# Scaling half-finished softmax rows on GpSimd instead of VectorE in three attention stages of a four-layer backbone

## The reference, cut to what matters

```python
# layer 0: 16 query heads, 4 key/value heads; context queries see context keys only
s = einsum("bkgqd,bkld->bkgql", q, k) * scale
o = einsum("bkgql,bkld->bkgqd", softmax(s), v)
...
# layer 1: 8 heads, two softmax maps each
s1 = einsum("bhqd,bhld->bhql", q1, k[0]) * scale
s2 = einsum("bhqd,bhld->bhql", q2, k[1]) * scale
p = softmax(s1) - lam * softmax(s2)
o = einsum("bhql,bhle->bhqe", p, v)
...
# layer 3: 16 heads, latent queries only, a relative-position bias on the latent keys
p = softmax(concatenate([s_nb + bias, s_c], axis=-1))
```

## Time and profile before

| what | value |
|---|---|
| median of three runs | 2454.05 us (2451.64 to 2458.83) |
| span of the profiled execution, first to last instruction | 2459.1 us |
| mean granted TensorE clock | 0.982 of full speed |
| PE busy | 2342.6 us (95%) |
| DVE busy | 1694.4 us (69%) |
| ACT busy | 1132.1 us (46%) |
| POOL busy | 334.6 us (14%) |
| attention stage of layer 0 | about 143 to 229 us |
| attention stage of layer 1 | about 816 to 902 us |
| attention stage of layer 3 | about 2154 to 2221 us |

### The profile page before, as it was taken

The page is one execution under the profiler, slowest core; times in us unless marked ns, Lnnn a source line. Parts: engine busy times, 40 slices in busy tenths (PEclk is TensorE's granted clock), DMA queues, the critical chain, the costliest instruction groups (busy, mean ns, idle before and its releaser), DMA issues.

```text
span 2459.1 us, 35614 instructions
## 1 busy us (share of the span) xinstructions
PE 2342.6 (95%) x13806; PEld 1911.9 (78%) x13806; DVE 1694.4 (69%) x2573; ACT 1132.1 (46%) x1948; POOL 334.6 (14%) x266
## 2 busy tenths in 40 slices
PE   5999999999999999999999998899999999978998
PEld 3765788888888558888878777778888888847998
DVE  2376689987444776999865236768999834486874
ACT  3466554432332666443324444455343325386663
POOL 0000411111100003111112003332111011002110
PEclk8999999999999999999999999999999999999999
DMA  8621645556233022555552420044555636403664
GB/s 255 200 69 58 192 138 163 163 150 203 79 91 94 27 79 78 165 162 158 172 168 72 120 77 27 2 138 119 159 159 161 201 92 122 145 10 112 182 183 132
DMA packets 458426, 312.26 MB, mean 127 GB/s; under 512 B 24258, under 2 KB 413810, under 8 KB 458004
## 3 DMA queue, kind: packets, MB, share of 16 engines
q1 hardware_dynamic: 455488, 308.44, 42.8%
q10 hardware_dynamic: 2772, 1.56, 0.2%
HBM read 308.92 MB, written 1.05 MB: 126 GB/s over the span
## 4 chain that ended last, share of the span: by engine, by line
PE 83%; DVE 7%; ACT 4%; DMA 3%; issue 2%; SPq 1%; DVEq 0%; ACTq 0%
PE bank L1652 72%; PE bank L1945 2%; PE bank L1895 2%; DMA slab_raw<-in_mod_w 1%; PE bank L1915 1%; DVE stat L1281 1%; DVE slab_lo L1015 1%; ACT p L767 1%; ACT hb L586 1%; DMA slab_raw<-in_a_w_o 1%; DVE q_part L1340 1%; PE bank L1726 1%; ACT slab_hi L571 1%; SPq L536 1%; ACT pt L779 1%
## 5 line engine op out<-in xcount | busy, mean ns | idle before, releaser
L1652 PE MATMUL bank<-h_hi,slab_hi 128*128 128x512 f32 (+1 forms) x2416 | 844.3, 349 | 25.5 <-DVE slab_lo L1015 17.9
L1652 PE MATMUL bank<-h_lo,slab_hi 128*128 128x512 f32 (+1 forms) x2416 | 833.9, 345 | 0.0
L1652 PE MATMUL bank<-h_hi,slab_lo 128*128 128x512 f32 (+1 forms) x2416 | 833.6, 345 | 0.0
L1015 DVE TENSOR_TENSOR slab_lo<-slab_raw,slab_hi 128x1024 fp32r<-128x1024 f32 (+1 forms) x388 | 522.7, 1348 | 309.8 <-ACT slab_hi L571 308.6
L571 ACT ACTIVATE slab_hi<-slab_raw 128x1024 fp32r<-128x1024 f32 (+1 forms) x388 | 400.7, 1034 | 313.7 <-PE bank L1652 228.4
L1652 PEld LDWEIGHTS bank<-h_hi,slab_hi 128*128 128x128 f32 x2416 | 463.5, 192 | 102.9 <-issue 42.6
L1652 PEld LDWEIGHTS bank<-h_lo,slab_hi 128*128 128x128 f32 x2416 | 463.9, 192 | 53.2 <-issue 0.5
L1652 PEld LDWEIGHTS bank<-h_hi,slab_lo 128*128 128x128 f32 x2416 | 463.4, 192 | 53.7
L989 ACT ACTIVATE conv<-bank,prm 128x512 f32<-128x512 f32 (+1 forms) x176 | 127.7, 726 | 447.4 <-PE bank L1652 447.3
L1040 DVE SCALAR_TENSOR_TENSOR mod_sum<-slab_raw,cond_wide,mod_sum 128x512 f32<-128x512 f32 x420 | 317.6, 814 | 0.3 <-DMA slab_raw<-in_mod_w 0.3
L1652 PE MATMUL bank<-g_hi,slab_hi 128*128 128x512 f32 (+1 forms) x770 | 268.3, 348 | 2.1 <-ACT res_t L623 2.1
(11 more groups left out here) (242 smaller groups left out, 2657.6 us busy)
## 6 DMA issues: line engine op xcount, KB each, us to landing
slab_raw<-in_ffn_w_up SPq DMA_DIRECT2D x176, 512.0 KB, 3.9
slab_raw<-in_mod_w SPq DMA_DIRECT2D x168, 512.0 KB, 4.6
slab_raw<-in_ffn_w_down SPq DMA_DIRECT2D x64, 512.0 KB, 3.7
slab_gap<-in_mod_w SPq DMA_DIRECT2D x24, 512.0 KB, 7.9
slab_raw<-in_ffn_w_down SPq DMA_DIRECT2D x32, 384.0 KB, 3.2
slab_raw<-in_b_w_qkv SPq DMA_DIRECT2D x24, 512.0 KB, 3.7
slab_raw<-in_c_w_in SPq DMA_DIRECT2D x24, 512.0 KB, 3.8
slab_raw<-in_d_w_qkv SPq DMA_DIRECT2D x24, 512.0 KB, 4.1
```

What stands on the lines that cost most here:

```text
L1015: nc.vector.tensor_tensor(wlo[slot][:, 0:w], raw[of][:, 0:w], whi[slot][:, 0:w].bitcast(f32), ALU.subtract).then_inc(s_lo, 1)
L1652: ins = mm(out, l, r, start=first and n == 0, stop=last and n == 2)
```

## The change

DVE still forms all reciprocals. The multiplication of `p1` by its reciprocal goes to POOL for layer 0's context units (32 of 64), for all units of layer 1 (the first map, 32 units), and for the odd units of layer 3 (16 of 32). The reciprocal signals `inverted`, POOL waits for it, multiplies in place and signals `p_scaled`. In layers 0 and 3 PE waits for `p_scaled` in place of `p_ready` for such units. In layer 1 the last DVE step of a unit (`p1 = p2 * factor + p1`) waits for `p_scaled` and moves from iteration `w + 1` to iteration `w + 2`; `p_ready` comes from it as before. In POOL's queue the new instructions stand ahead of the residual's sums of the same layer.

```diff
+        def scaled_by_pool(i):
+            U = attention_units(i)
+            return [w for w in range(len(U)) if i == 1 or (i == 0 and U[w][1] == 0) or (i == 3 and w % 2)]
...
                         dve.wait_ge(S["exped"], maps * (w + 1))
-                        link(nc.vector.reciprocal(stat[:, 4:4 + maps, w], stat[:, 2:2 + maps, w]))
-                        r1 = stat[:, 4, w:w + 1]
-                        if maps == 1:
-                            nc.vector.tensor_scalar(p1[w % MAPS][:, 0:nk], p1[w % MAPS][:, 0:nk], r1, None,
-                                                    ALU.mult).then_inc(S["p_ready"], 1)
+                        inverse = nc.vector.reciprocal(stat[:, 4:4 + maps, w], stat[:, 2:2 + maps, w])
+                        if w in by_pool:
+                            inverse.then_inc(S["inverted"], 1)
                         else:
-                            nc.vector.tensor_scalar(p1[w % MAPS][:, 0:nk], p1[w % MAPS][:, 0:nk], r1, None, ALU.mult)
-                            link(nc.vector.tensor_tensor(stat[:, 5, w:w + 1], stat[:, 5, w:w + 1], small[:, 13:14],
-                                                         ALU.mult))
-                            nc.vector.scalar_tensor_tensor(p1[w % MAPS][:, 0:nk], p2[w % MAPS][:, 0:nk],
-                                                           stat[:, 5, w:w + 1], p1[w % MAPS][:, 0:nk],
-                                                           ALU.mult, ALU.add).then_inc(S["p_ready"], 1)
+                            link(inverse)
+                            nc.vector.tensor_scalar(p1[w % MAPS][:, 0:nk], p1[w % MAPS][:, 0:nk], stat[:, 4, w:w + 1],
+                                                    None, ALU.mult).then_inc(S["p_ready"], 1)
+                        if maps == 2:
+                            dve.wait_ge(S["inverted"], w + 1)
+                            step.up(nc.vector.tensor_tensor(stat[:, 5, w:w + 1], stat[:, 5, w:w + 1], small[:, 13:14],
+                                                            ALU.mult))
+                            weighted[w] = step.n
+                    w = u - 2
+                    if maps == 2 and 0 <= w < len(U):
+                        nk = CTX if U[w][1] == 0 else T
+                        dve.wait_ge(s_dve, weighted[w])
+                        dve.wait_ge(S["p_scaled"], w + 1)
+                        nc.vector.scalar_tensor_tensor(p1[w % MAPS][:, 0:nk], p2[w % MAPS][:, 0:nk],
+                                                       stat[:, 5, w:w + 1], p1[w % MAPS][:, 0:nk],
+                                                       ALU.mult, ALU.add).then_inc(S["p_ready"], 1)
...
+            def scale_units(i):
+                S, U = att[i], attention_units(i)
+                for n, w in enumerate(scaled_by_pool(i)):
+                    nk = CTX if U[w][1] == 0 else T
+                    pool.wait_ge(S["inverted"], n + 1)
+                    nc.gpsimd.tensor_scalar(p1[w % MAPS][:, 0:nk], p1[w % MAPS][:, 0:nk], stat[:, 4, w:w + 1], None,
+                                            ALU.mult).then_inc(S["p_scaled"], 1)
...
                     if 0 <= w < len(U):
-                        pe.wait_ge(S["p_ready"], w + 1)
+                        if maps == 1 and w in by_pool:
+                            pe.wait_ge(S["p_scaled"], by_pool.index(w) + 1)
+                        elif maps == 1:
+                            pe.wait_ge(S["p_ready"], w + 1 - sum(x < w for x in by_pool))
+                        else:
+                            pe.wait_ge(S["p_ready"], w + 1)
```

More of the change, by code:

```diff
@@ L348, in build_program @@
             att[i] = {n: sem(f"{n}_{i}") for n in (
-                "qk_ready", "swapped", "score_full", "biased", "context_copied", "negmax", "exped", "p_ready", "p_turned",
+                "qk_ready", "score_full", "negmax", "exped", "inverted", "p_scaled", "p_ready", "p_turned",
                 "pt_ready", "pv_full", "o_hi", "o_lo", "v_full")}
             if i < 2:
-                att[i].update({n: sem(f"{n}_{i}") for n in ("squared_h", "ss_full", "rs_ready", "o_normed")})
+                att[i].update({n: sem(f"{n}_{i}") for n in ("swapped", "squared_h", "ss_full", "rs_ready")})
+            if i == 1:
+                att[i]["o_normed"] = sem("o_normed_1")
+            if i == 3:
+                att[i].update({n: sem(f"{n}_{i}") for n in ("biased", "context_copied")})
         att[2] = {n: sem(f"gla_{n}") for n in (
@@ L1266, in attention @@
                     add_bias(0)
+                by_pool, weighted = scaled_by_pool(i), {}
                 for u in range(len(U) + TURN + 10):
@@ L1634, in _ @@
                     gla()
+                else:
+                    scale_units(i)
                 residual(2 * i)
@@ L1901, in turn_free @@
                         pe.wait_ge(S["rs_ready"], before[1] + 1)
+                by_pool = scaled_by_pool(i)
                 for u in range(-1, len(U) + TURN + 6):
```

## The result

The changed kernel took 2461.01 us (median of 20 runs, 2454.29 to 2467.81) beside 2455.97 us for the kernel before (20 runs, 2451.64 to 2460.56). The ratio of the two times is on record as 1.0016, 95% interval 1.0009 to 1.0024: slower by 3.9 us, between 2.2 and 5.9. That is within the 0.3% of the prediction and within its range, but the forecast was 2 us faster, and the interval excludes that.

A forecast was written before the change was run, and what follows sets the result against it. PE was taken to bound layer 0, DVE layer 1 and no engine layer 3. Layer 1's -2 us, with 0 for layers 0 and 3, took the median from 2454.05 to 2452 us; range 2446 to 2466.

The forecast's parts named there:

- Layer 3: 0: Layer 3's odd units: no change, POOL having 1.2 us before the transpose; gain bound 0.5, loss 0.8 us at 1.28.
- D: POOL's time for one multiplication, taken from a copy: 0.40 us at 256 and 0.61 at 512 elements.
- The start of the stage: Start of layer 3: DVE's freed step feeds ACT, which had work already; gain bound 0.5 us.
- signs of being wrong: A POOL multiplication over 0.8 us; a gap before a transposition put down to POOL in layers 0 or 3.
- rival 1: Layer 1: slow POOL multiplication holds DVE's multiply-add; some 13 us loss, 2467; chance 0.2 over 0.3%, 0.2 for 0 to +7.
- The bounds of D: POOL's multiplication lies between a copy (0.40, 0.61 us) and a two-input instruction (0.72, 1.28), at 256 and 512 elements.
- Forecast -1.3 to -2.7: Layer 1: 0.16 to 0.34 us less per head over 8 heads; -2 us taken.
- Held for nearly the whole of the first: POOL and DVE two-SBUF-input instructions exclude each other; layer 1's multiply-add goes as if started 0.13 us before POOL's end.
- The wait on `p_scaled` costs nothing: Layer 1: DVE's wait for POOL costs 0, as POOL is done a full iteration earlier.
- Layer 0: 0: Layer 0's context units: no change, PE's work covers it; gain bound -1.5 us, loss +2.6 if uncovered.
- Rival 3: Layer 1: `p_ready` an iteration later holds PE; +1.6 us, so 2454; chance 0.1.

The follow-up runs named there:

- l3_alone: Changed kernel with only layer 3's odd units on POOL, layers 0 and 1 as before: 2460.87 us, ratio 1.0019 to the kernel before.
- l3_even: Only layer 3's even units on POOL in place of the odd ones, layers 0 and 1 as before: 2457.38 us, ratio 1.0001 to the kernel before.
- l3_behind_scores: Only layer 3's units w = 3, 7, ... on POOL, half of the odd units: one execution, 2449.43 us, beside 2456.41 before; period 7.60.
- l3_before_pv: Only layer 3's units w = 1, 5, ... on POOL, half of the odd units: one execution, 2466.07 us, beside 2456.41 before; period 7.95.
- l3_two_inputs: Only layer 3's odd units on POOL, as tensor_tensor with the reciprocal spread as second input: one execution, 2455.56 us; period 7.61.
- l1_alone: Changed kernel with only layer 1's first maps on POOL, layers 0 and 3 as before: 2454.87 us, ratio 0.9997 to the kernel before.
- l0_alone: Changed kernel with only layer 0's context units on POOL, layers 1 and 3 as before: 2456.00 us, ratio 0.9994 to the kernel before.
- mixed_forms: POOL takes layer 1 with tensor_scalar and layer 3's units except w % 4 = 1 with tensor_tensor, layer 0 on DVE: 2456.13 us, ratio 1.0002 to before.

## Why the prediction was wrong, step by step

- **"Layer 3: 0" failed.** Its reasoning named the right transpose and the right margin (POOL has 1.2 us), and put a POOL time of 0.61 against it, with 1.28 as the bound and 0.8 us as the loss there. The term that was mis-sized is D: 1.56 us. Over the margin by about 0.3, once a period: 7.61 to 7.94 us, in the six full periods from 2166.22 to 2213.86 us 2.0 us. The start of the stage, for which the prediction had a gain of 0.5 at most and no loss, adds 1.6 (`l3_alone`, 15.09 us) to 1.75 us, in part through the clock. First scores to last value product: 64.44 us before, 68.09 in `l3_alone` (+3.7), where the timed runs give 2.0 to 7.1. Shown by three changes of it: the other units (`l3_even`, `l3_behind_scores`: no loss), that unit alone (`l3_before_pv`: all of it), a shorter instruction in the same unit (`l3_two_inputs`: period as before, start +0.9). The prediction's sentence that the odd units' transposes stand before the value product is right for every second one of them only; its sum counted eight in all, one a period, and that count came out.
- **Its signs of being wrong both came:** a POOL multiplication over 0.8 us, and a gap in front of a transpose in layer 3 put down to POOL. That the time still fell inside the range is luck: the range was held open upward by rival 1, whose loss was to come from DVE's waits in layer 1.
- **The bounds of D were no bounds.** They were a copy and a two-input instruction, on the reasoning that one tile input lies between or below. The remark in rival 1, that a scalar operand per partition is one more thing to read, pointed the right way and was set aside as "one column". By the cited loop of the Trainium skill ("GPSIMD Engine Reference", section "Elementwise — side-by-side cycle accounting") the estimate for 512 elements was 0.77 us. The page gives that loop as a best case; for this instruction the trace does not agree, and the measurement decides: 1.56.
- **Layer 1: the size was about right, the mechanism only half.** Forecast -1.3 to -2.7 (0.16 to 0.34 a head); a head shrank by 0.44, from 10.42 to 9.98 us, and `l1_alone` measured -0.7, between -3.2 and +1.5. "Held for nearly the whole of the first" did not hold for `tensor_scalar`: DVE lost 0.46 of 1.56. Had it, rival 1's steps with 0.92 and 1.56 us would have grown by 2 x (0.52 + 0.95) = 2.94 us, to a head of 12.9 and a loss of 20 us. It nearly holds for `tensor_tensor` (0.80 of 1.04), which is also the instruction in the earlier trace rows from which the rule was read. "The wait on `p_scaled` costs nothing" failed too: DVE waited 3.2 us for it in all, once a head. Errors of opposite sign, D too small and the hold too long, gave a sum of the right order by luck.
- The Trainium skill, "SBUF — State Buffer", section "Who interferes with whom", calls the shared ports an exclusive lock and says, of VectorE's two-port modes, that whoever issues first gets them for the whole instruction. The prediction carried this over to the multiply-add. The `tensor_tensor` rows (0.80 of 1.04 us) come near it, 870.51 and 870.53 above (0.46 of 1.56) do not.
- **Layer 0: 0** held (PE 68.41 of 70 us; `l0_alone` -3.7 to +0.7 us). **Rival 3**, the late `p_ready`, is there only at the start of layer 1 (821.22, 823.54 and 833.25), with 1.38, 1.25 and 0.60 us of idle; what it costs was not measured by itself.
- **What stays open.** The parts don't quite give the whole. In layer 3, first scores to last value product took 64.44 us before, 66.56 after and 68.09 in `l3_alone`: +2.1 or +3.7 (before has a low-clock stretch at the stage's end, 0.71 from 2214 to 2218 us). In layer 1, the first to the last norm product took 61.61 us before (839.47 to 901.08) and 59.44 after (841.23 to 900.67), -2.2; from the stage's first scores to the first of them it took 24.31 before (815.16 to 839.47), 25.70 after (815.53 to 841.23) and 24.19 in `l1_alone` (814.90 to 839.09), so +1.4 or -0.1. Together -0.2 to +2.9, where 2.2 to 5.9 was measured. A gain goes missing in `mixed_forms` in the same way: layers 1 and 3 are together 3.7 us shorter in its profiled execution (first scores to last norm product 83.35 us beside 85.92, first scores to last value product 63.30 beside 64.44), and its time is not. The granted clock goes along with both: its mean over the timed runs is 0.9824 for the changed kernel (20 runs) and 0.9837 for `mixed_forms` (12), against 0.9847 (35) and 0.9851 (17) for runs of the kernel before beside the experiments, each uncertain by about 0.0005. Over the 94 runs of the kernel before beside the experiments, 0.001 less of the clock goes with 0.83 us more (0.5 to 1.4 for single chips); by that the changed kernel's clock is worth an estimated 1.9 us and that of `mixed_forms` 1.2. But `l3_even` has 0.9834 and no loss that can be measured. Whether the new gaps in PE's work bring the low clock about was only argued from this; no run isolates it.

## What to carry to other kernels

Before work moves to another engine, find a row of that very instruction form there, since neighbouring forms are no bound: here the form decided both the duration (1.56 against 1.04 us) and how long the other engine was held (0.46 against 0.80). Compare it with the margin of each consumer, not with busy shares: in layer 3 the even units and every second odd one took the slow instruction with no longer period, and the one whose transpose stood in front of the value product carried the loss. Look at the start of a stage by itself, where no earlier work covers a consumer: here it cost as much as the growth of five periods. Moved work that relieves a full engine is worth only the distance to the next limit (0.44 of 10.42 us a head here, then ACT and PE stand in the way).

## What the runs showed of the hardware

- POOL's `tensor_scalar` with a scalar column: 0.92 us for 256 and 1.56 us for 512 float32 elements. `tensor_tensor` with that column spread as second input: 0.61 and 1.04 us, faster than with two full tiles (0.72 and 1.28) and faster than the one-input form.
- A DVE instruction with two SBUF inputs that starts 0.02 to 0.04 us behind POOL is held 0.46 us by a `tensor_scalar` of 1.56, or not at all, and 0.80 us by a `tensor_tensor` of 1.04, every time. A DVE `tensor_scalar` that starts 0.93 us into the former still takes 0.92 instead of 0.49 us, so the hold is not just at its beginning.
- Which of the two is held is not seen from the starts and changes from head to head in one execution: with DVE 0.02 us behind in both, POOL at 860.54 (1.85 us) and DVE at 870.53 (0.94).
